# The second attention's filling matmuls in passes of 384 columns and two PSUM banks, with VectorE's order changed

## The chip, the cores and the metric
The kernel runs on one core of one Trainium2 chip. The metric is device time in microseconds (us). The engines are TensorE (PE), VectorE (DVE), ScalarE (ACT), GpSimd (POOL) and SyncE (SP); each runs its own instructions in order and waits for the others by semaphores. PSUM, where TensorE writes its products, has eight banks of 512 fp32 columns.

## The reference
Two layers of a diffusion backbone over 512 latent tokens and 256 context tokens, 1024 wide. Each layer runs three token mixers on one modulated input, merges them by sigmoid gates, projects, and then runs a SwiGLU. The part that matters is mixer B, a neighbourhood attention of eight heads of 64 with a learned bias, and context keys in the same softmax:

```
qa, ka, va, qb, kb, vb, uc, gz = jnp.split(h @ w_in, IN_SPLITS, axis=-1)
s_nb = jnp.einsum('bqhd,brqjhd->bhqrj', q_r, k_win).astype(jnp.float32) * scale
s_nb = s_nb + bias[None].astype(jnp.float32)
s_ctx = jnp.einsum('bqhd,bshd->bhqs', q_r, kc).astype(jnp.float32) * scale
s = jnp.concatenate([s_nb.reshape(B, H, GRID_W, kr * kcn), s_ctx], axis=-1)
p = jax.nn.softmax(s, axis=-1).astype(v.dtype)
y = ga * (oa @ w_branch[0]) + gb * (ob @ w_branch[1]) + gf * (oc @ w_branch[2])
```

The last layer has no output for the context, so there queries and gates are 512 tokens wide, and keys still 768.

## The kernel before
Products keep fp32's precision by parts: each operand is split into a high part (fp32r) and the rest, the low part, and three matmuls stand for one. A weight unit is 128 output columns; ScalarE makes its high part (line 587), GpSimd its low part (line 513).

The second attention (`attention` with `branch == 1`) is a loop of slots. A slot n is one head and one pair of query tiles: three slots a head in layer 0 (two with latent queries and one with context queries, `ORDER`), two in layer 1. "Odd" and "even" head mean its number. In a slot TensorE does, in this order:
- the scores of slot n + 1 into banks 0 to 3 (line 2005), for its first and its second query tile;
- the turn (transpose) of slot n's probabilities in up to three groups, into banks 4 and 3 in turn (line 2036). The first group waits for GpSimd's `p_ready`, the product of the exponentials with the inverse row sums (line 525);
- half of the slot's filling matmuls (`fill`, line 2091), a last small turned group, the output products (line 2055), the other half of the filling matmuls, and the output product of the last group.

The filling matmuls work off eight weight units beside the attention: six are queries and keys of the coming heads, alternately (0, 2, 4 queries, 1, 3, 5 keys), the last two are gates. A 768-wide unit takes 24 steps of two matmuls, 384 columns into bank 6 and 384 into bank 7; a 512-wide one takes 24 matmuls into bank 6. One unit is spread over three slots in layer 0 and two in layer 1. The first matmul of a unit waits until the one before is read out: ScalarE writes the high parts (`query_parts`, line 747, or `key_parts`, line 755) and VectorE the low parts (`query_rest`, line 1422, or `key_rest`, line 1431) from the same banks.

In a slot ScalarE also takes half of the output out of PSUM (`move_half`, line 893), the high parts of the turned groups (`turned_hi`, line 870), the exponentials of slot n + 1 (`probs`, line 862), and for odd heads the output's high part (`out_hi`, line 900), whose low part GpSimd makes between its two products (`o_rest`, line 533). At the end of a slot in which a unit ended it splits a weight unit, and after a key unit it copies the key rows to the other half of the partitions (`key_copies`, line 763). The scores of the first slot of each second head wait for these copies and for the low parts. Then it starts the bias transfer of the next head. VectorE does the fold of the output (`fold`, line 1518), the maxima of slot n + 1 (`maximum`, lines 1465 to 1479), the low parts of the turned groups (`turned_lo`, line 1493) and the inverses of the row sums (line 1486).

The order of each engine is written out by hand in the loop over n; no scheduler moves it.

## Time and profile before

| | us |
|---|---|
| median of 3 runs | 2493.85 |
| lowest, highest | 2493.56, 2496.89 |
| the profiled execution | 2498.33 |
| its span, first to last instruction | 2496.5 |
| TensorE busy in the span | 2315.2 (93%) |
| second attention, layer 0 | 548 to 722 of the span |
| second attention, layer 1 | 1845 to 1984 of the span |

The profile is one execution. A row of waits says who waited, for whom, and for how long. A row of the timeline says when an instruction (or a few alike) began, how long it took, and in brackets how long its engine had been idle and who ended that. Matmuls overlap, so the start of the next tells more than the length. PE's granted clock is given as a share of full speed.

### The profile page before, as it was taken

The numbers are of one execution on the slowest core, as the hardware profiler recorded it, in microseconds if no ns is written. First come the engines' busy times: TensorE is split into PE (matmuls) and PEld (weight loads), VectorE is DVE, ScalarE is ACT, GpSimd is POOL, SyncE is SP. The second block draws the span as 40 slices with busy tenths as digits, with TensorE's granted clock in tenths as the row PEclk, the third lists the DMA queues.
The fourth block names the chain that finished last, engine by engine and source line by source line (L and its number), as shares of the span: only waits on it lengthen the run. The fifth ranks groups of instructions, "written<-read, shape, count | busy, mean of one in ns | idle before, by whom it ended". The sixth has DMA issues, their size and how long they took to land. (4 is left out here: it accounts for less than half of the span.)

```text
span 2496.5 us, 34770 instructions
## 1 busy us (share of the span) xinstructions
PE 2315.2 (93%) x13090; PEld 2107.2 (84%) x13090; DVE 1222.7 (49%) x2548; ACT 949.3 (38%) x1852; POOL 1088.3 (44%) x844
## 2 busy tenths in 40 slices
PE   6989999998899989999999979899998898999997
PEld 2879888987789989999999868778877788988887
DVE  5786266565543474663831274546635526311124
ACT  3222366435541562111111244256535536422223
POOL 1333255434443544333532433446434456644545
PEclk9989999999999999999999989999999999999999
DMA  6541100132112535443522533121222245533335
GB/s 244 193 139 51 51 26 26 43 137 58 58 45 74 181 130 190 134 154 107 171 90 67 161 101 122 54 64 35 65 67 66 66 152 161 152 94 99 110 117 170
DMA packets 117935, 263.86 MB, mean 106 GB/s; under 512 B 13348, under 2 KB 13604, under 8 KB 116136
## 3 DMA queue, kind: packets, MB, share of 16 engines
q1 hardware_dynamic: 108000, 233.89, 29.6%
q10 hardware_dynamic: 9800, 28.19, 3.4%
q8 instruction: 82, 1.34, 0.2%
q14 instruction: 53, 0.43, 0.1%
HBM read 251.53 MB, written 10.49 MB: 105 GB/s over the span
## 5 line engine op out<-in xcount | busy, mean ns | idle before, releaser
L513 POOL TENSOR_TENSOR w_lo<-raw,w_hi 128x512 fp32r<-128x512 f32 x632 | 864.8, 1390 | 1031.2 <-ACT w_hi L587 1030.6
L587 ACT ACTIVATE w_hi<-raw 128x512 fp32r<-128x512 f32 x632 | 366.8, 626 | 682.8 <-PE ps L1747 251.1
L525 POOL TENSOR_TENSOR p_sb<-p_sb,row_inv 128x768 f32<-128x768 f32 (+2 forms) x160 | 185.3, 1168 | 300.7 <-DVE row_inv L1486 300.0
L1745 PE MATMUL ps<-h_hi,w_lo 128*128 128x384 f32 (+1 forms) x864 | 311.4, 360 | 1.2 <-DVE h_lo L1244 1.2
L1745 PE MATMUL ps<-h_lo,w_hi 128*128 128x384 f32 (+1 forms) x864 | 311.1, 360 | 0.0
L1745 PE MATMUL ps<-h_hi,w_hi 128*128 128x384 f32 (+1 forms) x864 | 311.1, 360 | 0.0
L1576 DVE TENSOR_TENSOR ps<-silu_g,ps 128x768 f32<-128x768 f32 (+3 forms) x52 | 37.8, 726 | 379.4 <-PE ps L1747 177.5
L1745 PEld LDWEIGHTS ps<-h_hi,w_lo 128*128 128x128 f32 x864 | 162.2, 188 | 17.3 <-DVE h_lo L1244 1.4
L1745 PEld LDWEIGHTS ps<-h_lo,w_hi 128*128 128x128 f32 x864 | 162.2, 188 | 16.0
L1745 PEld LDWEIGHTS ps<-h_hi,w_hi 128*128 128x128 f32 x864 | 162.2, 188 | 15.9
L2091 PE MATMUL ps<-h_hi,w_lo 128*128 128x384 f32 (+1 forms) x408 | 134.3, 364 | 27.1 <-DVE k_ll L1431 14.8
L1747 PE MATMUL ps<-h_hi,w_hi 128*128 128x384 f32 x456 | 152.3, 334 | 0.0
L1747 PE MATMUL ps<-h_lo,w_hi 128*128 128x384 f32 x456 | 152.3, 334 | 0.0
L1747 PE MATMUL ps<-h_hi,w_lo 128*128 128x384 f32 x456 | 152.3, 334 | 0.0
L870 ACT ACTIVATE pt_hi<-ps 128x512 fp32r<-128x512 f32 (+1 forms) x208 | 114.3, 550 | 97.7 <-PE ps L2036 96.3
L1104 DVE SCALAR_TENSOR_TENSOR ada_unused_gate_up<-ada_raw_gate_up,ada_cond_gate_up 128x1024 bf16<-128x1024 f32 x96 | 143.2, 1491 | 5.3 <-DMA ada_raw_gate_up<-in_w_ada 0.3
L1493 DVE TENSOR_TENSOR pt_lo<-ps,pt_hi 128x512 fp32r<-128x512 f32 (+1 forms) x208 | 129.5, 624 | 21.6 <-ACT pt_hi L870 20.3
L862 ACT ACTIVATE p_sb<-ps,neg_max 128x768 f32<-128x768 f32 (+2 forms) x160 | 120.4, 753 | 35.6 <-DVE neg_max L1479 19.1
L2091 PE MATMUL ps<-h_lo,w_hi 128*128 128x384 f32 (+1 forms) x408 | 132.0, 359 | 0.0
L2091 PE MATMUL ps<-h_hi,w_hi 128*128 128x384 f32 (+1 forms) x408 | 131.9, 358 | 0.0
L2036 PE MATMUL ps<-ident,p_sb 128*128 128x128 f32 x736 | 108.8, 280 | 20.2 <-DVE pt_lo L1493 16.7
L2036 PEld LDWEIGHTS ps<-ident,p_sb 128*128 128x128 f32 x736 | 84.8, 141 | 42.8 <-DVE pt_lo L1493 36.3
(219 smaller groups left out, 5474.4 us busy)
## 6 DMA issues: line engine op xcount, KB each, us to landing
raw<-in_stream SPq DMA_DIRECT2D x632, 256.0 KB, 2.8
ada_raw_gate_up<-in_w_ada SPq DMA_DIRECT2D x48, 512.0 KB, 3.6
ada_raw_fourier_in<-in_w_ada SPq DMA_DIRECT2D x24, 512.0 KB, 4.4
bias_sb<-in_bias ACTq DMA_DIRECT2D x32, 320.0 KB, 3.0
first_raw<-in_w_first SPq DMA_DIRECT2D x8, 1152.0 KB, 5.2
scratch<-xr ACTq DMA_DIRECT2D x16, 512.0 KB, 3.8
xr<-scratch SPq DMA_DIRECT2D x14, 512.0 KB, 4.9
ln_rows<-in_norm_rows SPq DMA_DIRECT2D x8, 512.0 KB, 5.2
```

The lines of the kernel that those rows point to most:

```text
L513: nc.gpsimd.tensor_tensor(w_lo[:, u % 2, cols], raw[:, u % 2, cols], w_hi[:, u % 2, cols].bitcast(F32), ALU.subtract).then_inc(S("lo_made" ...
L525: nc.gpsimd.tensor_tensor(p, p, row_inv[:, c:c + 1].broadcast_to([P, keys]), ALU.mult).then_inc(S("p_ready"), 1)
L587: nc.scalar.activation(w_hi[:, s, cols], raw[:, s, cols], ACT.Copy).then_inc(S("hi_made"), 1)
L862: nc.scalar.activation(p_sb[branch][n % 2][i][:, 0:keys], region(branch, i, 0, keys), ACT.Exp, bias=neg_max[:, i:i + 1], accum_out=row_sum ...
L870: nc.scalar.activation(pt_hi[branch][:, a:a + w], ps[:, TURN_BANK[branch] + order % 2, 0:w], ACT.Copy).then_inc(S("hi_out"), 1)
L1104: nc.vector.scalar_tensor_tensor(ada_unused[kind][:, :], ada_raw[kind][:, s, :], 1.0, ada_cond[kind][:, c, :], ALU.mult, ALU.mult, accum_o ...
L1493: nc.vector.tensor_tensor(pt_lo[branch][:, a:a + w], ps[:, TURN_BANK[branch] + order % 2, 0:w], pt_hi[branch][:, a:a + w].bitcast(F32), AL ...
L1576: nc.vector.tensor_tensor(up, shaped(silu_g[:, c, 0:w]), up, ALU.mult).then_inc(S("hidden"), 1)
L1745: last = nc.tensor.matmul(bank(0), tile, x[:, k, 0:split], start=start, stop=stop)
L1747: last = nc.tensor.matmul(bank(1), tile, x[:, k, HALF:TOK], start=start, stop=stop)
L2036: last = nc.tensor.transpose(ps[:, TURN_BANK[branch] + order % 2, col:col + P], p_sb[branch][n % 2][i][:, a:a + P], ident[:, :])
L2091: last = nc.tensor.matmul(ps[:, bank, 0:b - a], tile, x[:, k, a:b], start=r == 0, stop=r == FILL_STEPS - 1, skip_group_check=True)
```

## The change
- The unit's work is cut into passes (`fill_passes`): a 768-wide unit is two passes of 24 matmuls with 384 columns, a 512-wide one stays one pass. The number of matmuls stays as it was; a unit's weight tiles are now gone through once for each pass. Pass after pass the bank alternates between 6 and 7 (`pass_bank`), and the first matmul of a pass waits for the pass before the last.
- High and low parts are taken for each pass (64x384 instead of 64x768), the first pass's at a time of its own: `first_pass_ended` tells in which slot, "late" in layer 0 (behind everything else of the slot) and "early" in layer 1.
- VectorE's order in the second attention becomes: first maximum, low part of the first turned group, fold, low part of the second group, second maximum, first inverse, low parts of a pass, second inverse, last group, a late pass.
- ScalarE takes a pass's high parts ahead of `move_half`, and `out_hi` moves from before the second exponential to behind the last turned group.

The first attention (`branch == 0`) keeps its order and its passes.

```
+                    if branch == 1:
+                        if n + 1 < count:
+                            maximum(n + 1, 0)
+                        turned_lo(n, 0)
+                        if n:
+                            fold(n - 1)
+                        for g in groups[1:2]:
+                            turned_lo(n, g)
+                        if n + 1 < count:
+                            maximum(n + 1, 1)
+                            invert(n + 1, 0)
+                        if f is not None:
+                            fill_rest(f, len(fill_passes(ph, f)) - 1)
+                        if early is not None:
+                            fill_rest(early, 0)
+                        if n + 1 < count:
+                            invert(n + 1, 1)
+                        for g in groups[2:]:
+                            turned_lo(n, g)
+                        if late is not None:
+                            fill_rest(late, 0)
+                        continue
...
                     if f is not None:
-                        fill_out(f)
+                        fill_out(f, len(fill_passes(ph, f)) - 1)
+                    if early is not None:
+                        fill_out(early, 0)
+                    if branch == 1 and n:
+                        move_half(n - 1)
...
                     for g in groups[2:]:
                         turned_hi(n, g)
+                    if branch == 1 and n and (n - 1) // pairs % 2:
+                        out_hi(n - 1)
                     for name in slot_pieces(ph, n):
                         piece(*name)
+                    if late is not None:
+                        fill_out(late, 0)
...
                         if r == 0:
-                            if f or half:
-
-                                pe.wait_ge(S("fill_out"), at(ph, "fill_out") + fill_halves(ph) * f + half)
+                            held = 2 if branch == 1 else 1
+                            if m >= held:
+
+                                pe.wait_ge(S("fill_out"), at(ph, "fill_out") + m - held + 1)
                                 if branch == 1:
-                                    pe.wait_ge(S("fill_lo"), at(ph, "fill_lo") + min(f, 6))
+                                    pe.wait_ge(S("fill_lo"), at(ph, "fill_lo") + min(m - held + 1, passes_to(ph, 6)))
...
-                            runs = ((6, 0, HALF), (7, HALF, TOK)) if wide else ((6, 0, LAT),)
-                        for bank, a, b in runs:
-                            last = nc.tensor.matmul(ps[:, bank, 0:b - a], tile, x[:, k, a:b], start=r == 0, stop=r == FILL_STEPS - 1,
-                                                    skip_group_check=True)
+                        last = nc.tensor.matmul(ps[:, bank, 0:b - a], w[:, u % 2, k * P:(k + 1) * P], x[:, k, a:b], start=r == 0,
+                                                stop=r == FILL_STEPS - 1, skip_group_check=True)
...
+def fill_passes(ph, f):
+
+    if ph.tiles > LT or ph.part and f < 6 and f % 2:
+        return ((0, HALF), (HALF, TOK))
+    return ((0, LAT),)
+
+def passes_to(ph, f):
+
+    return sum(len(fill_passes(ph, n)) for n in range(f))
+
+def pass_bank(ph, f, i):
+
+    return FILL_BANK[ph.part] + (passes_to(ph, f) + i) % 2 if ph.part else FILL_BANK[0]
+
+def first_pass_ended(ph, n, late):
+
+    f, part = divmod(n + 2, ph.tiles // 2)
+    if part == 1 and f < FILLS and len(fill_passes(ph, f)) == 2 and late == (ph.tiles > LT):
+        return f
+    return 0 if n == 0 and not late and len(fill_passes(ph, 0)) == 2 else None
```

VectorE in layer 0, the slot in which a key unit has just ended, before. `k_ll_115` holds the keys' low parts, `o_sum_117` the folded output, `max_c` and `neg_max` the maxima:

```order
L1518 TENSOR_TENSOR o_sum_117<-ps,o_half_119 64x256 [waits moved]
L1431 TENSOR_TENSOR k_ll_115<-ps,k_hh_113 64x768 [waits fill_out]
L1431 TENSOR_TENSOR k_ll_115<-ps,k_hh_113 64x768
L1476 TENSOR_REDUCE max_c<-ps 128x1 [waits scored]
L1479 TENSOR_SCALAR neg_max<-max_c 128x1 [waits max_part]
L1476 TENSOR_REDUCE max_c<-ps 128x1 [waits scored]
L1479 TENSOR_SCALAR neg_max<-max_c 128x1 [waits max_part]
L1493 TENSOR_TENSOR pt_lo_131<-ps,pt_hi_129 128x512 [waits hi_out]
L1486 RECIPROCAL row_inv<-row_sum 128x1 [waits probs]
L1493 TENSOR_TENSOR pt_lo_131<-ps,pt_hi_129 128x512 [waits hi_out]
L1486 RECIPROCAL row_inv<-row_sum 128x1 [waits probs]
L1493 TENSOR_TENSOR pt_lo_131<-ps,pt_hi_129 128x128 [waits hi_out]
```

The same slot of the changed kernel, on the same engine:

```order
L1476 TENSOR_REDUCE max_c<-ps 128x1 [waits scored]
L1479 TENSOR_SCALAR neg_max<-max_c 128x1 [waits max_part]
L1493 TENSOR_TENSOR pt_lo_131<-ps,pt_hi_129 128x512 [waits hi_out]
L1518 TENSOR_TENSOR o_sum_117<-ps,o_half_119 64x256 [waits moved]
L1493 TENSOR_TENSOR pt_lo_131<-ps,pt_hi_129 128x512 [waits hi_out]
L1476 TENSOR_REDUCE max_c<-ps 128x1 [waits scored]
L1479 TENSOR_SCALAR neg_max<-max_c 128x1 [waits max_part]
L1486 RECIPROCAL row_inv<-row_sum 128x1 [waits probs]
L1431 TENSOR_TENSOR k_ll_115<-ps,k_hh_113 64x384 [waits fill_out]
L1431 TENSOR_TENSOR k_ll_115<-ps,k_hh_113 64x384
L1486 RECIPROCAL row_inv<-row_sum 128x1 [waits probs]
L1493 TENSOR_TENSOR pt_lo_131<-ps,pt_hi_129 128x128 [waits hi_out]
```

The keys' low parts moved from ahead of the maxima to between the inverses, and the second maximum from ahead of both low parts of the turned groups to behind them.

ScalarE in that slot, before (`k_hh_113` the keys' high parts, `p_sb` the probabilities, `pt_hi_129` the turned ones):

```order
L893 ACTIVATE o_half_119<-ps 64x256 [waits folded,attended]
L755 ACTIVATE k_hh_113<-ps 64x768 [waits unit_done]
L755 ACTIVATE k_hh_113<-ps 64x768
L870 ACTIVATE pt_hi_129<-ps 128x512 [waits turned_p]
L862 ACTIVATE p_sb_126,row_sum<-ps,neg_max 128x256 [waits turned_p,max_ready]
L870 ACTIVATE pt_hi_129<-ps 128x512 [waits turned_p]
L900 ACTIVATE o_sb<-o_sum_117 128x256 [waits folded]
L862 ACTIVATE p_sb_127,row_sum<-ps,neg_max 128x256 [waits turned_p,max_ready]
L870 ACTIVATE pt_hi_129<-ps 128x128 [waits turned_p]
L587 ACTIVATE w_hi<-raw 128x512 [waits raw_ready10,unit_done]
L587 ACTIVATE w_hi<-raw 128x512 [waits raw_ready11]
L763 ACTIVATE k_hh_113<-k_hh_113 64x768 [waits fill_out]
```

And of the changed kernel (its lines 754, 892, 869, 861, 899 and 762 are the old 755, 893, 870, 862, 900 and 763):

```order
L754 ACTIVATE k_hh_113<-ps 64x384 [waits unit_done]
L754 ACTIVATE k_hh_113<-ps 64x384
L892 ACTIVATE o_half_119<-ps 64x256 [waits folded,attended]
L869 ACTIVATE pt_hi_129<-ps 128x512 [waits turned_p]
L861 ACTIVATE p_sb_126,row_sum<-ps,neg_max 128x256 [waits turned_p,max_ready]
L869 ACTIVATE pt_hi_129<-ps 128x512 [waits turned_p]
L861 ACTIVATE p_sb_127,row_sum<-ps,neg_max 128x256 [waits turned_p,max_ready]
L869 ACTIVATE pt_hi_129<-ps 128x128 [waits turned_p]
L899 ACTIVATE o_sb<-o_sum_117 128x256 [waits folded]
L587 ACTIVATE w_hi<-raw 128x512 [waits raw_ready10,unit_done]
L587 ACTIVATE w_hi<-raw 128x512 [waits raw_ready11]
L762 ACTIVATE k_hh_113<-k_hh_113 64x768 [waits fill_out]
```

The output's high part moved behind the last turned group; the splitting of the weights and the key copies still stand behind all of it. GpSimd's order is unchanged.

## Rows read from the trace of the kernel before

**Rows 1.** Line 2091, the filling matmuls: what ended their idle time (us, times).
```profile
  DVE k_ll L1431: 14.8, 6
  DVE q_st L1422: 11.6, 6
```
**Rows 2.** Timeline of PE, layer 0: turns of seven slots (start, length, us).
```profile
608.85 1.04 PE L2036 MATMUL ps<-ident,p_sb 128*128 128x128 f32 x8
618.27 0.60 PE L2036 MATMUL ps<-ident,p_sb 128*128 128x128 f32 x4
624.20 1.03 PE L2036 MATMUL ps<-ident,p_sb 128*128 128x128 f32 x8
630.11 1.04 PE L2036 MATMUL ps<-ident,p_sb 128*128 128x128 f32 x8
640.84 0.60 PE L2036 MATMUL ps<-ident,p_sb 128*128 128x128 f32 x4
646.99 1.09 PE L2036 MATMUL ps<-ident,p_sb 128*128 128x128 f32 x8
653.03 1.04 PE L2036 MATMUL ps<-ident,p_sb 128*128 128x128 f32 x8
```
**Rows 3.** Timeline of PE, layer 1: turns of five slots, and of the last two.
```profile
1869.23 1.03 PE L2036 MATMUL ps<-ident,p_sb 128*128 128x128 f32 x8
1880.08 1.04 PE L2036 MATMUL ps<-ident,p_sb 128*128 128x128 f32 x8
1886.75 1.03 PE L2036 MATMUL ps<-ident,p_sb 128*128 128x128 f32 x8
1896.60 1.04 PE L2036 MATMUL ps<-ident,p_sb 128*128 128x128 f32 x8
1904.36 1.04 PE L2036 MATMUL ps<-ident,p_sb 128*128 128x128 f32 x8
...
1972.54 1.03 PE L2036 MATMUL ps<-ident,p_sb 128*128 128x128 f32 x8
1977.74 1.97 PE L2036 MATMUL ps<-ident,p_sb 128*128 128x128 f32 x8 [0.83 <-POOL p_sb L525]
```
**Rows 4.** Timeline of all engines, layer 0, one slot of an odd head.
```profile
602.80 1.09 PE L2036 MATMUL ps<-ident,p_sb 128*128 128x128 f32 x8
603.50 0.60 ACT L870 ACTIVATE pt_hi<-ps 128x512 fp32r<-128x512 f32 x1 [2.58 <-PE ps L2036]
603.60 0.41 DVE L1465 TENSOR_REDUCE max_c<-ps 128x1 f32<-128x256 f32 x1
...
604.65 0.60 ACT L870 ACTIVATE pt_hi<-ps 128x512 fp32r<-128x512 f32 x1
604.65 0.21 DVE L1473 TENSOR_SCALAR neg_max<-max_a,max_c 128x1 f32<-128x1 f32 x1
...
605.43 0.81 ACT L862 ACTIVATE p_sb<-ps,neg_max 128x640 f32<-128x640 f32 x1
605.45 0.67 DVE L1493 TENSOR_TENSOR pt_lo<-ps,pt_hi 128x512 fp32r<-128x512 f32 x1
...
606.36 0.17 DVE L1486 RECIPROCAL row_inv<-row_sum 128x1 f32<-128x1 f32 x1 [0.24 <-ACT p_sb L862]
606.61 0.73 POOL L533 TENSOR_TENSOR o_sb<-o_sum,o_sb 128x256 fp32r<-128x256 f32 x1
...
607.31 1.25 POOL L525 TENSOR_TENSOR p_sb<-p_sb,row_inv 128x640 f32<-128x640 f32 x1
```
**Rows 5.** Tile k_ll: low parts of the first attention (ns: least, median, most).
```profile
L1508 DVE TENSOR_TENSOR k_ll<-ps,k_hh x16: 417/556/695, 297.4 to 1687.1; 64x512 fp32r<-64x512 f32 x8, 64x256 fp32r<-64x256 f32 x8
```
**Rows 6.** Timeline of ACT and PE, layer 0, a key unit's copies and the scores.
```profile
681.66 1.70 ACT L763 ACTIVATE k_hh<-k_hh 64x768 fp32r<-64x768 f32 x2
683.46 0.48 PE L2005 MATMUL ps<-k_hh,q_st 128*128 128x256 f32 x2 [0.71 <-issue]
```
**Rows 7.** A stretch behind a fill wait: PE, PEld, DVE, ACT, POOL busy, clock.
```profile
590.80:594.60 3.80, 3.80 (x18) 3.57 (x17) 1.84 (x6) 3.76 (x11) 2.96 (x4) 0.55 0.30 84
```

More of the change, by code:

```diff
@@ L942, in attention @@
                     f = fill_ended(ph, n - 1)
-                    if n:
+                    early, late = (first_pass_ended(ph, n, late) if branch == 1 else None for late in (False, True))
+                    if branch == 0 and n:
                         move_half(n - 1)
                     if f is not None:
-                        fill_out(f)
+                        fill_out(f, len(fill_passes(ph, f)) - 1)
[3 more added lines that the diff above has]
+                        move_half(n - 1)
                     turned_hi(n, 0)
@@ L951, in attention @@
                         turned_hi(n, g)
-                    if fill_halves(ph) == 2 and (n + 1) % pairs == 0 and n + 1 < count:
-                        gate_half((n + 1) // pairs, 0)
-                    if n and (n - 1) // pairs % 2:
+                    if branch == 0 and ph.tiles > LT and (n + 1) % pairs == 0 and n + 1 < count:
+                        fill_out((n + 1) // pairs, 0)
+                    if branch == 0 and n and (n - 1) // pairs % 2:
                         out_hi(n - 1)
@@ L1430, in key_rest @@
                     rows, n = slice(HD * x, HD * x + HD), 2 * (c % 2) + x
-                    last = nc.vector.tensor_tensor(halves(k_ll[1][rows, n, :], TOK), product(qk_bank(c, 1), TOK, rows),
-                                                   halves(k_hh[1][rows, n, :].bitcast(F32), TOK), ALU.subtract)
+                    last = nc.vector.tensor_tensor(halves(k_ll[1][rows, n, a:b], w), product(bank, w, rows),
+                                                   halves(k_hh[1][rows, n, a:b].bitcast(F32), w), ALU.subtract)
                 last.then_inc(S("fill_lo"), 1)
@@ L1540, in attention @@
                     f = fill_ended(ph, n - 1)
+                    early, late = (first_pass_ended(ph, n, late) if branch == 1 else None for late in (False, True))
+                    if branch == 1:
[20 more added lines that the diff above has]
+                        continue
                     if n:
                         fold(n - 1)
[L1543 to L1548 removed]
                     if n + 1 < count:
```

111 lines of the change are left out of this document (48 added, 63 removed).

## The prediction
> **What bounds the kernel now.** I read the shares of busy time first, then who waits for whom in the second attention alone, then its instructions in order of time, since only those tell which wait ends last. Over the whole program TensorE is busy 93%, so most stages have nothing to give. In the second attention it is not: there the filling matmuls are released late by VectorE's low parts, six times 14.8 us in all for keys and six times 11.6 us for queries [rows 1]. These 26.4 us are what the change can take away at its source, and no more than that can come from this edit.
>
> The stage runs in slots, one per head and pair of query tiles: scores of the next slot, turns of this slot's probabilities, half of the filling matmuls, output products, the other half. I measure a slot from one turn's start to the next. In layer 0 a head has three slots: 9.42, 5.93 and 5.91 us for a head with an even number and 10.73, 6.15 and 6.04 for an odd one [rows 2]. In layer 1 four slots make a period: 10.85, 6.67, 9.85 and 7.76 us [rows 3]. The long ones are those in which a new unit starts.
>
> **The fill wait (gone).** With two banks in turn, a pass needs the pass before the last to be read out, and that happened most of a slot ago. ScalarE's and VectorE's reading of the last pass lies beside this slot's matmuls. So TensorE's idle time at the fill goes in all 12 places. I take it whole; the question is what is late next.
>
> **The new order's chain.** Before, VectorE did both maxima first and the low parts after. Now the second maximum stands behind both low parts, and the second half of the probabilities behind it on ScalarE. From one slot [rows 4], laid in the new order from the turn's start: 0.70 to the first high part, 1.15 to the second's start, 0.60 for it, 0.67 for its low part, 1.26 for the second maximum (603.60 to 604.86), 0.93 from the second exponential's start to the inverse, 0.15 and 0.08 to GpSimd, 1.25 for its product, 0.06 to the next turn. That is 6.85, about 6.8 us, since an instruction begins a little before the one ahead ends. Where the high part of the output is due, it now stands behind the last turned group: 0.4 on ScalarE and 0.7 on GpSimd, queued ahead of the second product there (the order of GpSimd's queue has not moved), so 7.8 us. Before, such a slot took 5.9 to 6.1 us, because nothing of the second maximum hung on the turn. This is a loss of 0.9 to 1.8 us in each slot that had no fill wait to lose.
>
> **The low parts of a pass.** 64x512 takes 695 ns and 64x256 417 [rows 5], so 64x384 should take 556 and a pass of two 1.1 us. It stands between the two inverses. In slots with context keys it is covered. In the last slot of an even head in layer 0 VectorE still has 0.4 us of the late pass's low parts to do when the slot begins, so the first maximum moves and the slot takes 7.3 instead of 6.8.
>
> **The key copies.** ScalarE doubles a unit's key rows at the end of the slot, behind the splitting of a weight unit. The scores of the next head pair wait for it. In the trace this already ends last: the copies end at 683.36 and the scores start at 683.46, with 0.71 us idle before [rows 6]. The change moves them little: second exponential at about 4.4 us (3.7 in layer 0, whose next scores are the short context ones), 0.9 to the end of the last high part, 1.2 of splitting, 1.7 of copies, so they end at 8.2 (7.5). Then 0.1 and the scores' 1.1 (four pairs like the row at 683.46): the slot takes 9.4 in layer 1 and 8.75 in layer 0. That is the wait that takes the place of the fill's in each key unit.
>
> **The sum, layer 0.** Even head: first slot 6.5 (TensorE's own work: the third slot's 5.91, and 0.6 since the next scores are the long ones; so the fill wait was 2.9), second 5.95 (GpSimd's product just in time), third 7.3; 19.75 against 21.26, so -1.5, three times -4.5. Odd head: 8.75, 6.75 (5.95 and the output's high part), 7.75; 23.25 against 22.92, so +0.3, three times +1.0. The very first slot and the last two heads have no fill wait to lose, yet pay the chain: I take +4.2, of which the last short slots are the larger part, as in layer 1 below. Sum +0.7 us.
>
> **The sum, layer 1.** 10.85 becomes 9.4, 6.67 becomes 7.8, 9.85 becomes 7.9 (chain with output) and 7.76 becomes 7.7 (TensorE's work, the last low part just late): 32.8 against 35.13, -2.3, three times -7.0. The end has slots without filling work: 5.20 us between the last turns [rows 3] becomes 7.0, and two before it lose 0.3 each: +2.4. Sum -4.6 us.
>
> Together -3.9 us. The profiled execution took 2498.33 us (span 2496.5), 4.5 above the median of the runs, 2493.85; its own sum gives 2494.4, which is 2490 beside the median. Of the 26.4 us taken away some 22 come back, 6 at the key copies and the rest along the chain of the second maximum. A measurement of this kernel can tell about 0.2% (5 us) from no change, so this is "the same", 2488.9 to 2498.8.
>
> **The clock.** Just behind the fill wait of an odd head TensorE's granted clock fell to 0.55 for 3.8 us [rows 7], that is mostly the lower of its two levels. An odd head's first slot took 10.73 instead of 9.42 [rows 2], so such a stretch costs 1.3 us. I count three of them in the two stages. My sum lets these stretches vanish with the waits. The longest idle time that I leave is some 2.1 us, ahead of the scores behind the key copies.
> The Trainium skill (TensorE: Matmul & The Clock Gate, section "A second HAM failure mode: psum-queue depth-cycling") tells of a kernel that cycles through PSUM banks, in which many short idle times between groups of matmuls made the clock fall and rise over and over. By that rule this change, which trades few long waits for many short ones, is the wrong way round, and its case is the third rival. That short waits do it no row here shows: in the rows the fall follows a long one.
>
> **Rivals.**
> First, the late chain is hidden and only the key copies stay: slots then run at TensorE's work. For it speaks that my chain adds handoffs one by one, each read from a slot in which something else may have been waited for. Against it: GpSimd's product is needed whole before the turn and already ends 0.06 us ahead of it in odd heads. It gives 2493.85 - 26.4 + 9 (six key copies at 1.5) = 2476.
> Second, on the other side, the second maximum costs more than I read. It is ahead of both the exponential and the product in about 34 of 40 slots. Each 0.25 us that the low parts, the fold between them or the start of the maximum add per slot is 8.5 us: 2490 + 8.5 = 2498.5, and at 0.4 us it is 2504. It decides from 0.26 us a slot on. For it: the first low part cannot begin before the first maximum has ended, and where the maximum waits for a bias transfer the whole chain moves. Against it: all its pieces are read with their handoffs, from a slot in which only GpSimd's product ended late.
> Third, the clock falls in each of the 12 units, where before three stretches were slow in these stages: and my sum let those vanish. Twelve at 1.3 us are 15.6: 2490 + 16 = 2506.
> Fourth, the change does not do what it says, since the pass before the last is not yet read out when a new one starts. Then the fill waits stay and the chain is paid in full: 2493.85 + 22 = 2516. Against it: the first pass of a unit ends a whole slot before the next unit begins.
>
> **How the numbers follow.** The forecast has 0.45, and alone it reaches from 2482 to 2498 (0.2 us a slot either way on 40 slots): 0.17 of its chance lies below 2488.9, 0.24 within, 0.04 above. The first rival has 0.23, all faster. The second has 0.18, of which 0.04 is within. The third has 0.11 and the fourth 0.03, both slower. That is 0.40 faster, 0.28 the same and 0.32 slower. The time is the forecast's, 2490. The range holds the forecast, most of the first rival and the second, and the near part of the third: 2473 to 2507.
>
> **What would show it.** Right: in the waits of the second attention no filling matmul waits for q_st or k_ll; turns wait for GpSimd's p_sb in most slots, and scores for the copies of k_hh (about 2 us, six times); an odd head's slots in layer 0 add up to some 23 us, an even one's to 20, a period in layer 1 to 33. Wrong: turns seldom wait for p_sb and the periods shrink to TensorE's work (first rival); slots of 7.3 or more everywhere (second); a granted clock under 0.95 in both stages (third); fill waits still there (fourth). All other stages must keep their times within 1 us.

## The result and the profile after

| | us |
|---|---|
| before, median of 7 runs | 2494.06 (2492.42 to 2500.57) |
| changed, median of 7 runs | 2504.86 (2501.92 to 2507.62) |
| ratio, 95% interval | 1.0037 [1.0026, 1.0049] |
| forecast | 2490.0 (2473 to 2507) |
| changed, the profiled execution, its span | 2501.92, 2500.1 |
| TensorE busy in the span | 2330.5 (93%) |

The changed kernel is slower by 10.8 us, where the forecast was 4 us faster. The profiled executions are only 3.6 us apart in span, since that of before lies 4.3 us above its median and that of the changed kernel 2.9 below its own. So stages are compared below, not spans.

**The wait is gone.** These are rows from the page's list of costliest groups. The filling matmuls (now line 2109) have 0.7 us of idle time ahead of them in the whole program, and none of it for k_ll or q_st [rows 1]. The line of the exponential (861, before 862) has become the one that waits. Changed kernel:

```profile
L2109 PE MATMUL ps<-h_hi,w_lo 128*128 128x384 f32 (+1 forms) x408 | 149.3, 366 | 0.7 <-ACT gates_a L911 0.7
L861 ACT ACTIVATE p_sb<-ps,neg_max 128x768 f32<-128x768 f32 (+2 forms) x160 | 120.3, 752 | 76.6 <-DVE neg_max L1473 58.2
```
The same line of ScalarE in the kernel before:
```profile
L862 ACT ACTIVATE p_sb<-ps,neg_max 128x768 f32<-128x768 f32 (+2 forms) x160 | 120.4, 753 | 35.6 <-DVE neg_max L1479 19.1
```
The exponentials' idle time went from 35.6 to 76.6 us. That is the late second maximum, read in one row; m2 below, which moves it alone, has 7.6.

**The slots, layer 0.** Turns of the changed kernel on TensorE, to be laid beside [rows 2]; the start of one less that of the one ahead is a slot:

```profile
601.09 1.10 PE L2060 MATMUL ps<-ident,p_sb 128*128 128x128 f32 x8 [1.36 <-POOL p_sb L525]
609.01 1.09 PE L2060 MATMUL ps<-ident,p_sb 128*128 128x128 f32 x8 [1.04 <-POOL p_sb L525]
615.68 0.60 PE L2060 MATMUL ps<-ident,p_sb 128*128 128x128 f32 x4
621.65 1.09 PE L2060 MATMUL ps<-ident,p_sb 128*128 128x128 f32 x8 [0.43 <-POOL p_sb L525]
629.11 1.09 PE L2060 MATMUL ps<-ident,p_sb 128*128 128x128 f32 x8
638.43 1.05 PE L2060 MATMUL ps<-ident,p_sb 128*128 128x128 f32 x4
646.03 1.09 PE L2060 MATMUL ps<-ident,p_sb 128*128 128x128 f32 x8 [1.47 <-POOL p_sb L525]
```
An even head is 6.67, 5.97 and 7.46 us (20.1; before 21.26), an odd one 9.32, 7.60 and 7.92 (24.8; before 22.92); the 7.92 ends with the turn at 653.95, shown further down. Turns now wait for GpSimd's product, as the bracket says.

**The slots, layer 1**, beside [rows 3]:

```profile
1868.69 1.04 PE L2060 MATMUL ps<-ident,p_sb 128*128 128x128 f32 x8
1876.09 1.04 PE L2060 MATMUL ps<-ident,p_sb 128*128 128x128 f32 x8
1885.47 1.04 PE L2060 MATMUL ps<-ident,p_sb 128*128 128x128 f32 x8
1893.38 1.09 PE L2060 MATMUL ps<-ident,p_sb 128*128 128x128 f32 x8 [0.46 <-POOL p_sb L525]
1901.22 1.10 PE L2060 MATMUL ps<-ident,p_sb 128*128 128x128 f32 x8
...
1975.78 1.03 PE L2060 MATMUL ps<-ident,p_sb 128*128 128x128 f32 x8
1982.58 1.97 PE L2060 MATMUL ps<-ident,p_sb 128*128 128x128 f32 x8 [0.60 <-POOL p_sb L525]
```
A period is 7.40, 9.38, 7.91 and 7.84: 32.5 us, before 35.1.

**One slot in order of time**, from 601.09 to 609.01, beside [rows 4]; start and length in us:

```profile
602.42 0.69 DVE L1493 TENSOR_TENSOR pt_lo<-ps,pt_hi 128x512 fp32r<-128x512 f32 x1
603.14 0.43 DVE L1518 TENSOR_TENSOR o_sum<-ps,o_half 64x256 f32<-64x256 f32 x1
603.68 0.69 DVE L1493 TENSOR_TENSOR pt_lo<-ps,pt_hi 128x512 fp32r<-128x512 f32 x1
604.29 0.41 DVE L1465 TENSOR_REDUCE max_c<-ps 128x1 f32<-128x256 f32 x1
...
605.59 0.80 ACT L861 ACTIVATE p_sb<-ps,neg_max 128x640 f32<-128x640 f32 x1 [1.94 <-DVE neg_max L1473]
...
606.50 0.17 DVE L1486 RECIPROCAL row_inv<-row_sum 128x1 f32<-128x1 f32 x1 [0.88 <-ACT p_sb L861]
606.53 0.41 ACT L899 ACTIVATE o_sb<-o_sum 128x256 fp32r<-128x256 f32 x1
...
607.02 0.73 POOL L533 TENSOR_TENSOR o_sb<-o_sum,o_sb 128x256 fp32r<-128x256 f32 x1 [0.28 <-ACT o_sb L899]
...
607.71 1.25 POOL L525 TENSOR_TENSOR p_sb<-p_sb,row_inv 128x640 f32<-128x640 f32 x1
```
The second exponential begins 4.50 us behind the turn (the chain said 4.4), and GpSimd's second product, ready to go at 606.7, starts at 607.71 behind the output's sum. The slot is 7.92; the chain said 7.8.

**The waits in layer 1** (1868 to 1984 us), in all, times, longest:

```profile
ACT p_sb L861 <- DVE neg_max L1473: 27.3, 14, 2.0
DVE max_c L1465 <- DMA bias_sb<-in_bias: 10.2, 7, 1.7
PE ps L2029 <- issue: 5.5, 3, 1.8
```
Layer 0 has the first and the last of these alike (27.0 and 5.5 us), and no wait for the bias transfer. The last is the scores behind the key copies. In time, beside [rows 6]:

```profile
1882.54 1.70 ACT L762 ACTIVATE k_hh<-k_hh 64x768 fp32r<-64x768 f32 x2
1884.33 0.47 PE L2029 MATMUL ps<-k_hh,q_st 128*128 128x256 f32 x2 [1.84 <-issue]
```

**The clock.** The windows run from a layer's first turn to 12 us behind its last; the pairs are busy time of PE, PEld, DVE, ACT and POOL, and the last three numbers are granted clock, DMA share and GB/s. Before, then changed:

```profile
558.90:731.07 172.17, 143.55 (x919) 133.41 (x918) 99.96 (x295) 96.72 (x225) 71.73 (x75) 0.98 0.18 52
1852.30:1989.74 137.44, 114.71 (x686) 101.47 (x685) 78.63 (x232) 78.25 (x172) 59.42 (x55) 0.95 0.22 65
```
```profile
557.24:736.12 178.88, 152.02 (x899) 135.17 (x898) 101.46 (x304) 97.70 (x235) 72.38 (x74) 0.94 0.17 50
1860.94:1994.58 133.64, 117.14 (x685) 101.93 (x684) 80.83 (x237) 77.89 (x178) 59.80 (x54) 0.95 0.23 67
```
Length times the missing share of the clock is 3.4 + 6.9 = 10 us before and 10.7 + 6.7 = 17 after (each clock is rounded to 0.01, so each product is good to 1 us). Five of the seven us more are lost behind layer 0's last turn (12 us at 0.57). The same 12 us before and in the changed kernel:

```profile
722.00:734.00 12.00, 12.00 (x71) 12.00 (x70) 7.87 (x9) 4.78 (x7) 3.44 (x4) 1.00 0.16 48
```
```profile
722.00:734.00 12.00, 8.70 (x32) 8.11 (x33) 2.00 (x5) 6.76 (x14) 5.57 (x7) 0.57 0.14 45
```
From the last turn to the next stage's first gate product, before and changed, is 7.1 us (719.07 to 726.14) and 10.5 (724.12 to 734.64):

```profile
726.14 0.96 DVE L1405 TENSOR_TENSOR ps<-gate_b,ps 128x768 f32<-128x768 f32 x1 [3.33 <-PE ps L1747]
```
```profile
734.64 0.96 DVE L1404 TENSOR_TENSOR ps<-gate_b,ps 128x768 f32<-128x768 f32 x1 [5.44 <-PE ps L1771]
```

### The profile page after: what moved, and what is told of

Same layout as the page of the kernel before. It is cut to its first block and busy times, and to the rows that moved or that the text cites. A ratio compares the mean times of both kernels' runs of the same rounds, so it can differ in the third digit from the quotient of the medians.

```text
span 2500.1 us, 34819 instructions
## 1 busy us (share of the span) xinstructions
PE 2330.5 (93%) x13090; PEld 2113.3 (85%) x13090; DVE 1230.2 (49%) x2566; ACT 952.0 (38%) x1872; POOL 1086.3 (43%) x844
## 5 line engine op out<-in xcount | busy, mean ns | idle before, releaser
L1769 PE MATMUL ps<-h_hi,w_lo 128*128 128x384 f32 (+1 forms) x864 | 311.4, 360 | 1.2 <-DVE h_lo L1243 1.2
L1769 PE MATMUL ps<-h_lo,w_hi 128*128 128x384 f32 (+1 forms) x864 | 311.1, 360 | 0.0
L1769 PE MATMUL ps<-h_hi,w_hi 128*128 128x384 f32 (+1 forms) x864 | 311.1, 360 | 0.0
L2109 PE MATMUL ps<-h_hi,w_lo 128*128 128x384 f32 (+1 forms) x408 | 149.3, 366 | 0.7 <-ACT gates_a L911 0.7
L861 ACT ACTIVATE p_sb<-ps,neg_max 128x768 f32<-128x768 f32 (+2 forms) x160 | 120.3, 752 | 76.6 <-DVE neg_max L1473 58.2
L2109 PE MATMUL ps<-h_lo,w_hi 128*128 128x384 f32 (+1 forms) x408 | 146.2, 358 | 0.0
L2109 PE MATMUL ps<-h_hi,w_hi 128*128 128x384 f32 (+1 forms) x408 | 146.1, 358 | 0.0
```

Source lines behind the costliest of these rows:

```text
L861: nc.scalar.activation(p_sb[branch][n % 2][i][:, 0:keys], region(branch, i, 0, keys), ACT.Exp, bias=neg_max[:, i:i + 1], accum_out=row_sum ...
L1769: last = nc.tensor.matmul(bank(0), tile, x[:, k, 0:split], start=start, stop=stop)
L2109: last = nc.tensor.matmul(ps[:, bank, 0:b - a], w[:, u % 2, k * P:(k + 1) * P], x[:, k, a:b], start=r == 0, stop=r == FILL_STEPS - 1, skip ...
```

## The experiments

Sixteen kernels (one of them the changed kernel again) in four groups of four, each group beside runs of the kernel before (medians 2494.64, 2495.66, 2496.25 and 2495.18). The table has the median, the ratio to before, the sum of the slots of both layers (first to last turn) and the clock lost, worked out as above.

| kernel | us | ratio, interval | slots | clock lost |
|---|---|---|---|---|
| before (first profile) | 2494.06 | | 285.6 | 10 |
| changed | 2504.86 | 1.0037 [1.0026, 1.0049] | 288.5 | 17 |
| a1 changed again | 2502.82 | 1.0028 [1.0018, 1.0037] | 289.3 | 19 |
| p1 passes only | 2491.37 | 0.9985 [0.9977, 0.9994] | 279.3 | 12 |
| m2 maxima first | 2468.02 | 0.9886 [0.9871, 0.9900] | 255.0 | 7 |
| k1 copies first | 2492.75 | 0.9989 [0.9981, 0.9998] | 279.1 | 10 |
| m1 late maximum | 2519.96 | 1.0101 [1.0086, 1.0115] | 307.6 | 21 |
| r1 old vector order | 2503.65 | 1.0034 [1.0021, 1.0047] | 291.6 | 15 |
| d1 bias early | 2501.12 | 1.0021 [1.0011, 1.0032] | 288.3 | 17 |
| b2 all three | 2464.38 | 0.9873 [0.9859, 0.9887] | 251.0 | 3 |
| f1 fold first | 2472.39 | 0.9913 [0.9899, 0.9927] | 261.4 | 5 |
| p2 old scalar order | 2473.33 | 0.9911 [0.9897, 0.9924] | 258.3 | 5 |
| e1 one low ahead | 2494.67 | 0.9999 [0.9988, 1.0009] | 281.3 | 9 |
| o1 output early | 2496.14 | 1.0003 [0.9992, 1.0013] | 281.6 | 13 |
| t1 end as before | 2500.23 | 1.0021 [1.0011, 1.0030] | 283.7 | 17 |
| h1 rests behind inverses | 2508.32 | 1.0056 [1.0043, 1.0070] | 294.3 | 14 |
| c3 only maximum late | 2485.20 | 0.9973 [0.9959, 0.9987] | 272.6 | 7 |
| b3 all four | 2466.51 | 0.9884 [0.9869, 0.9899] | 252.4 | 6 |

**p1.** The changed kernel, with VectorE's and ScalarE's old orders in the second attention:

```diff
-  maximum(n+1, 0); turned_lo(n, 0); fold(n-1); turned_lo(n, 1)
-  maximum(n+1, 1); invert(n+1, 0); fill_rest(...); invert(n+1, 1)
+  fold(n-1); fill_rest(...); maximum(n+1, 0); maximum(n+1, 1)
+  turned_lo(n, 0); invert(n+1, 0); turned_lo(n, 1); invert(n+1, 1)
```
ScalarE's old order is the one written out under p2.

> The changed kernel's passes and banks, with VectorE's and ScalarE's old order in the second attention (fold, a pass's low parts, both maxima, then the turned groups; output's high part before the second exponential). Theory A, the loss is the second maximum behind the low parts: the fill waits stay away and no chain comes in their place, so slots without a unit's start stay at 5.9 to 6.2 us, an even head in layer 0 takes 18.5 to 19, a period of four slots in layer 1 about 31, and the time is 2470 to 2480, 14 to 24 under the kernel before. Theory B, the passes themselves cost (twice the instructions for the parts, the changed order of the weight tiles): no faster than 2492. Theory C, TensorE's clock: fewer waits, so it must have less time at the lower level than the changed kernel.

It gained 3 us, far less than the 14 to 24 of theory A; theory B's bound was 2492. TensorE lost 12 us of clock and not 17, as theory C wanted. The fill wait is gone, but with two passes a unit's low parts come twice, and in the old order they stand ahead of the maxima. VectorE in layer 1, one slot:

```profile
1879.84 0.43 DVE L1514 TENSOR_TENSOR o_sum<-ps,o_half 64x256 f32<-64x256 f32 x1 [2.07 <-ACT o_half L892]
1881.06 1.39 DVE L1417 SCALAR_TENSOR_TENSOR q_st<-ps,q_st 64x512 fp32r<-64x512 f32 x2 [0.79 <-ACT q_st L746]
...
1884.86 0.68 DVE L1489 TENSOR_TENSOR pt_lo<-ps,pt_hi 128x512 fp32r<-128x512 f32 x1
```
The turn began at 1880.34, and its first low part only 4.5 us later; TensorE's second group waits 2.12 us for that. One slot of each period of four in layer 1 (7.43, 7.76 and 7.41 us before) takes 9.38 here.

**m2.** The changed kernel with one edit:

```diff
   maximum(n+1, 0)
+  maximum(n+1, 1)
   turned_lo(n, 0); fold(n-1); turned_lo(n, 1)
-  maximum(n+1, 1)
```


> The changed kernel with the second maximum put directly behind the first on VectorE, nothing else moved. Theory A: the second exponential and GpSimd's product come early again, turns no longer wait for p_sb, the first low part starts some 0.6 us later. 2478 to 2488. Theory B: at most 3 us under the changed kernel, 2501 to 2506.

35 to 37 us faster than the changed kernel (its two medians) and 1.1% faster than before: 10 us below the range of theory A. The exponentials' idle time fell from 76.6 to 7.6:

```profile
L861 ACT ACTIVATE p_sb<-ps,neg_max 128x768 f32<-128x768 f32 (+2 forms) x160 | 120.5, 753 | 7.6 <-DVE neg_max L1479 7.1
```
The same slot as above, in m2: the turn at 600.26, the second exponential 2.33 us behind it, the second product at +5.49 instead of +6.62:
```profile
600.26 1.09 PE L2060 MATMUL ps<-ident,p_sb 128*128 128x128 f32 x8
...
602.59 0.80 ACT L861 ACTIVATE p_sb<-ps,neg_max 128x640 f32<-128x640 f32 x1
...
605.75 1.25 POOL L525 TENSOR_TENSOR p_sb<-p_sb,row_inv 128x640 f32<-128x640 f32 x1
```

**k1.** The changed kernel with the copies ahead of the split:

```diff
+  key_copies(f // 2 + 1, ...)
   act.wait_ge(S("unit_done"), ph.unit + f + 1)
   split(ph.unit + f + 2, f % 2)
-  key_copies(f // 2 + 1, ...)
```

> The changed kernel with the key copies ahead of the splitting of the weight unit on ScalarE. If the scores' wait for the copies is what ends last in the six key slots, each gets 1.1 us shorter (odd heads of layer 0 from 24.8 to 23.7 us, periods in layer 1 from 32.6 to 31.5): 2497 to 2500. If the late chain behind it takes the place of the wait, no gain: 2503 to 2506.

A gain of 10 to 12 us against the changed kernel, about twice what was expected. The six waits are not gone but down from 1.8 us to 0.8:

```profile
1875.82 0.47 PE L2029 MATMUL ps<-k_hh,q_st 128*128 128x256 f32 x2 [0.80 <-issue]
```
Slots without slow clock give back the same 1.04 us (9.38 to 8.34 in layer 1, 8.79 to 7.75 in layer 0), as was expected: 6.2 in six. The slots give back 9.4 to 10.2 in all. The other 3 to 4 are stretches of lower clock: the changed kernel has five among its slots, k1 two. The copies were a bound, as the prediction said, and the clock came back on top.

**a1.** The changed kernel, unchanged, among the others.

> The changed kernel once more, for a second profile beside the others: 2503 to 2507. If the 4 us that the two profiles leave unexplained are the clock elsewhere, the stage in layer 0 again costs about 10 us more than before and that in layer 1 about 3.5 less, while the time at the lower clock in other stages differs.

2502.8, at the fast end of what was expected. Layer 0's stage, first turn to gate product, again costs 10.2 us more than before. Layer 1's costs 1.6 less and not 3.5, as the clock is low for 10.5 us behind its last turn, where the first profile has 7. The stretches of lower clock among the slots are again five, one of them at another place (609 us, where the first profile has 637).

**m1.** The kernel before, with the second maximum late on VectorE in the second attention. The first inverse moves with it, to where the changed kernel has it:

```diff
   maximum(n+1, 0)
-  maximum(n+1, 1)
   turned_lo(n, 0)
-  invert(n+1, 0)
   turned_lo(n, 1)
+  maximum(n+1, 1); invert(n+1, 0)
   invert(n+1, 1)
```

> The kernel before with one edit: in the second attention VectorE takes the second maximum of the next pair behind both low parts of the turned probabilities instead of directly behind the first maximum. Units stay one reading of 768 columns, nothing else moves. Theory A (the late second maximum is what makes the changed kernel slower, and does so by itself): the 25 or so slots without a wait for a unit's reading go from 5.9 to 6.8 us or more, the slots with such a wait absorb part of it: 2508 to 2520 us. Theory B (it costs only together with the passes' own work on VectorE): within 4 us of before, 2491 to 2498.

24 us slower than before, at the top of theory A's range: the late maximum costs without the passes too. The slots grew by 22 and the clock lost doubled from 10 to 21, so part of the 24 is slow clock. The first inverse's share was not run by itself. In the changed kernel it stays late in m2, which gains 35 us all the same.

**r1, f1.** Two VectorE orders between the changed kernel's with maxima first (m2) and p1's, with ScalarE's new order.

```diff
+  fold(n-1)                        # r1 and f1
+  fill_rest(...)                   # r1 alone
   maximum(n+1, 0); maximum(n+1, 1); turned_lo(n, 0)
+  invert(n+1, 0)                   # r1 alone
-  fold(n-1)                        # r1 and f1
   turned_lo(n, 1)
-  invert(n+1, 0)                   # r1 alone
-  fill_rest(...)                   # r1 alone
   invert(n+1, 1)
```

> The changed kernel with VectorE's old order (fold, rests of the pass, both maxima, then low parts) but ScalarE's new order. The kernel with the passes and both old orders took 2491.4 us, the changed one with both maxima first 2468.0. Theory A (VectorE's work ahead of the maxima, the fold and above all the rests of 1.1 to 1.4 us, took the 23 us between these two): 2487 to 2493. Theory B (ScalarE's order took them: output halves moved ahead of the first high part and the output's high part ahead of the second exponential): 2466 to 2473.

> The kernel with the passes and both maxima first (2468.0 us) with one edit on VectorE: the fold of the last output stands ahead of the maxima again, as in the kernel before; the passes' low parts stay between the two inverses. With the whole of VectorE's old order (fold and low parts of the pass ahead of the maxima) it took 2503.7, and there the fold waits 15 times, 55.9 us in all in layer 1, for ScalarE's first half of the output. Theory A (this wait, at the head of VectorE's queue, makes most of the 36 us between the two): 2485 to 2500. Theory B (the low parts of a pass, 1.1 to 1.4 us ahead of the maxima, make it): 2469 to 2476.

f1 is 4 us from m2, r1 36. So the fold at the head of the queue costs 4 us, though in r1's layer 1 it waits 55.9 us in all, and the low parts of a pass ahead of the maxima (with the first inverse early again) cost 31. The 4 us are near what the medians can tell (the intervals of f1 and m2 just meet), but the slots grow too, from 255.0 to 261.4. f1 is theory B; theory A had taken the largest wait in the list for the cause, and it was a place where VectorE waited anyway. r1 missed both its ranges, being 12 us above p1: ScalarE's new order is bad together with VectorE's old one.

**p2.** m2 with ScalarE's old order:

```diff
+  move_half(n-1)
   fill_out(...)
-  move_half(n-1)
   turned_hi(n, 0); probs(n+1, 0); turned_hi(n, 1)
+  out_hi(n-1)
   probs(n+1, 1); turned_hi(n, 2)
-  out_hi(n-1)
```

> The kernel with the passes and both maxima first (2468.0 us) with ScalarE's old order: first half of the output ahead of the pass's high parts, the output's high part ahead of the second exponential. Behind VectorE's old order this was worth -12 us (2491.4 against 2503.7), as the fold was then waited for. Theory A (only the fold at the head of VectorE's queue made ScalarE's order matter, and the fold is now behind the first low part): 2465 to 2471. Theory B (ScalarE's new order costs by itself): 2455 to 2461.

2473.3, in neither range: with the maxima first, ScalarE's new order is worth 5 us (first and third slot of an odd head in layer 0: 7.94 and 7.40 us, in m2 7.38 and 6.80).

**d1.** The changed kernel with the bias transfer earlier on ScalarE:

```diff
+  load_bias(ph, h + 1, j)
   fill_out(...); ...; split(...); key_copies(...)
-  load_bias(ph, h + 1, j)
```

> The changed kernel with one edit: ScalarE issues the transfer of the next head's bias at the start of the slot instead of at its end, behind split and key copies. In the trace of the changed kernel the maxima wait 7 times for this transfer in the layer with it, 10.2 us in all, and it takes 2.8 us to land. Theory A (those waits lie on the chain from maximum to turn): 2493 to 2498, against 2504 of the changed kernel. Theory B (the scores' second half or the low parts are ready no earlier than the bias, so the waits are hidden or change their name): 2501 to 2505.

2501.1, theory B: 2 to 4 us, at the edge of what can be told. The seven waits of 10.2 us are gone from the trace, but they had mostly covered others; layer 1's slots went from 121.6 to 121.3.

**b2.** The edits of m2, k1 and d1 together.

> The changed kernel with three edits together: both maxima ahead of the low parts, key copies ahead of the split of the weights, bias transfer issued at the slot's start. With the maxima alone it took 2468.0. Theory A (with the maxima early, the slots are bound by TensorE, and the scores wait only 2.6 us in all for key copies, the maxima once for a bias, 2.8 us): 2463 to 2467. Theory B (the edits add up as the copies did on the changed kernel, 10 to 12 us): 2452 to 2458.

2464.4, theory A, and the fastest of all, 1.3% under before. TensorE's clock does not fall at all in layer 1:

```profile
1838.56:1957.05 118.49, 112.00 (x691) 98.92 (x690) 78.52 (x239) 78.28 (x178) 60.81 (x55) 1.00 0.25 72
```

**e1.** The changed kernel with one low part less ahead of the second maximum:

```diff
   maximum(n+1, 0); turned_lo(n, 0); fold(n-1)
+  maximum(n+1, 1)
   turned_lo(n, 1)
-  maximum(n+1, 1)
```

> The changed kernel with the second maximum of VectorE behind the first low part and the fold, ahead of the second low part: half of the delay of the changed kernel, which took 2504, against 2468 with both maxima first. Theory A (each part of the chain counts as long as it is: the low part of 0.67 us ahead of the maximum is about half of what stands there): 2482 to 2490. Theory B (a threshold: up to some delay GpSimd's product is in time behind TensorE's work, so the first half costs little): 2468 to 2476.

2494.7, neither. Taking one low part away gives back 8 to 10 of 36 us; a low part and the fold still ahead of the maximum cost 27, three quarters of the whole. The expectation called this half of the delay, and it is more. In the slot shown for the changed kernel and m2 the second exponential starts 3.94 us behind the turn (598.46), where those have 4.50 and 2.33:

```profile
602.40 0.80 ACT L861 ACTIVATE p_sb<-ps,neg_max 128x640 f32<-128x640 f32 x1 [1.38 <-DVE neg_max L1473]
```
That is 74% of the way from m2 to the changed kernel, and 68% over all slots of both layers. The price goes roughly with the delay, once the delay is read where the exponential starts.

**o1.** The changed kernel with the output's high part where it was before:

```diff
+  out_hi(n-1)
   probs(n+1, 1); turned_hi(n, 2)
-  out_hi(n-1)
```

> The changed kernel with the output's high part on ScalarE ahead of the second exponential again. The prediction charged its new place, behind the last high part, with up to 1 us in the slots where it is due (GpSimd's sum of it stands ahead of the second product in its queue). Theory A (this charge is right, 12 to 16 such slots, some of them bound by other things): 2493 to 2499. Theory B (ahead of the exponential it costs ScalarE's chain its 0.4 us, and GpSimd's product is not late by the other way): 2501 to 2506.

7 to 9 us, theory A: the charge for its place was right.

**t1.** The changed kernel, maxima together in the last slots of each layer alone:

```diff
   maximum(n+1, 0)
+  if count - pairs - 2 <= n < count - 1: maximum(n+1, 1)
   turned_lo(n, 0); fold(n-1); turned_lo(n, 1)
-  maximum(n+1, 1)
+  if n < count - pairs - 2: maximum(n+1, 1)
```

> The changed kernel with the second maximum directly behind the first in the last four or five slots of each layer alone (the last of them have no filling work). In the changed kernel the last slots of layer 0 take 6.27, 5.96, 6.86 and 6.22 us against 6.35, 5.93, 5.91 and 4.36 before, and behind them TensorE's granted clock is at its lower level for 10.5 us, where before it did not fall. Theory A (the fall follows from the longer idle time ahead of the last turns): the slots give back 2.8 us in layer 0 and 2 in layer 1, the clock 3.4 more: 2494 to 2498. Theory B (the fall at the end of the stage comes anyway): 2499 to 2501, and the lower clock is seen at the end of layer 0 again.

2500.2, theory B. The last four slots of layer 0 give back 1.7 us (6.26, 5.95, 6.20 and 5.21 against 25.31 in all) and the last three of layer 1 2.0, but the clock falls behind layer 0 all the same:

```profile
722.00:729.50 7.50, 6.07 (x21) 6.07 (x22) 1.55 (x3) 4.26 (x7) 2.76 (x4) 0.54 0.25 72
```

**h1.** The changed kernel with a pass's low parts behind both inverses:

```diff
   invert(n+1, 0)
+  invert(n+1, 1)
   fill_rest(...)
-  invert(n+1, 1)
   turned_lo(n, 2)
```

> The changed kernel with the low parts of a pass (1.1 us on VectorE) behind the second inverse instead of between the two. Theory A (as the prediction said, in slots with context keys they are covered by the second exponential): 2501 to 2506. Theory B (they end behind the exponential, and the inverse and GpSimd's product wait for them in some dozen slots): 2492 to 2498.

2508.3, slower than both ranges. Layer 1's slots grew by 5 us (126.6 against 121.6). There the pass's low parts now run behind the inverse, so the turned low part of the slot's last group is late, and TensorE with it:

```profile
1881.84 1.10 DVE L1431 TENSOR_TENSOR k_ll<-ps,k_hh 64x384 fp32r<-64x384 f32 x2
...
1882.98 0.29 DVE L1493 TENSOR_TENSOR pt_lo<-ps,pt_hi 128x128 fp32r<-128x128 f32 x1
...
1883.32 0.33 PE L2079 MATMUL ps<-pt_lo,v_b 128*128 128x128 f32 x1 [1.53 <-DVE pt_lo L1493]
```
Between the inverses they were covered by the exponential all but 0.2 us, as the prediction had it: with them out of the way GpSimd's second product starts 5.49 us behind the turn at 1868 and not 5.66, and no turn had waited for it there.

**c3, b3.** c3 is the changed kernel with the edits of k1, d1 and o1; b3 is c3 with m2's edit too.

> The changed kernel with all that proved better but the second maximum: key copies ahead of the split, bias transfer at the slot's start, the output's high part ahead of the second exponential. Alone these gave 12, 3 and 8 us against the changed kernel's 2504. Theory A (they lie in different slots and add up): 2479 to 2484. Theory B (part of each was the same lower clock, that comes back only once): 2486 to 2491.

> The same with the second maximum directly behind the first too. With all of it but the output's high part it took 2464.4. Theory A (the output's sum on GpSimd ahead of the second product was late there as well): 2459 to 2462. Theory B (with the maxima early ScalarE is the one that is late, and the high part ahead of the second exponential costs its 0.4 us): 2465 to 2470. Against the kernel above, the late second maximum alone then costs 20 to 25 us by either.

b3 less c3 is 18.7 us: the late second maximum alone, with the other causes gone, where 20 to 25 was expected. Against the changed kernel c3 gives 20 where the three edits alone gave 12, 4 and 9, between the two theories. b3 is 2 us above b2, its theory B. The medians alone could not tell that, but the third slot of an odd head in layer 0 takes 7.40 and not 6.80 us: with the maxima first, the output's high part is better late.

## Why the prediction was wrong

**The fill wait goes** was right in all 12 places.

**The new order's chain** was right in its links: 4.50 us to the second exponential where 4.4 was said, slots of 7.92 where 7.8 was said, 5.97 where 5.95. By m1 it costs 24 us on the kernel before, where the prediction's fourth rival had 22; that they are so near is partly luck, since the 22 hold 6 of key copies and the 24 hold slow clock. That a pass's low parts are covered between the inverses (h1, all but 0.2 us) and the charge for the output's high part (o1) held too.

**The key copies** were right: 9.38 in layer 1 where 9.4 was said, 8.79 in layer 0 where 8.75 was.

**The sum, layer 1** was near: the slots took 3.8 us less than before, where -4.6 was said.

**The sum, layer 0** failed. It said +0.7 us. Measured from first turn to the next stage's gate product it is 177.4 us (557.24 to 734.64) against 167.2 (558.90 to 726.14): +10.2. Of the 9.5 us missed, 3.4 lie on the way from the last turn to the gate product, which my sum did not have at all. The three odd heads have 3.5 (24.59, 24.84 and 23.78 against 23.25), the three even ones 2.0 (20.08, 20.10 and 21.08 against 19.75). And 0.8 is mine: I took the odd heads of before at 22.92 each, and the two not in my rows were 22.77 and 22.23. The start and the last two heads were +3.9 (+4.2 said).

**The step that failed is the clock:** "My sum lets these stretches vanish with the waits." They did not: there are seven from the layers' first turns on, where before had four (the prediction counted three), and the clock lost went from 10 to 17 us. Four of the seven begin right at the scores behind the key copies, the very wait that the sum had kept as its longest. One of them, in the changed kernel:

```profile
636.75 0.47 PE L2029 MATMUL ps<-k_hh,q_st 128*128 128x256 f32 x2 [1.83 <-issue]
```
```profile
637.00:641.00 4.00, 4.00 (x19) 3.92 (x19) 1.86 (x6) 1.43 (x4) 0.74 (x1) 0.57 0.45 131
```
The clock over whole executions says the same as the two traces: its mean is 0.979 in 81 executions of the kernel before and 0.976 to 0.977 in 17 of the changed one, which is 6 to 7.5 us of 2500.

What a stretch costs is read between like slots of the changed kernel. The first two slots of an odd head are 9.07 and 7.60 or 9.32 and 7.60 with a stretch and 8.79 and 7.15 without, the first of an even head 7.67 with and 6.67 without. That is 0.7, 1.0 and 1.0 us, 2.7 in layer 0, and 3.4 more at its end: 6.1 of the 9.5 us are TensorE at the lower of its two levels. It is the third rival's mechanism at a part of its size. The 1.3 us of that rival was read between an odd and an even head. The kernel before has a third odd head without a stretch, 10.30 and 5.88 us in its first two slots, against 10.56 and 6.16 or 10.73 and 6.15 with one: 0.5 to 0.7. The chain itself is left with 0.5 us in an odd head (23.78 against 23.25) and 0.3 in an even one, 2.6 in six: too little to turn the sign by itself. Most of the odd head's is its second slot, 7.15 where 6.75 was said.

The 3.4 us at the end go with the clock in all eighteen profiles. The way from layer 0's last turn to the gate product takes 7.1 us in the two where the clock does not fall there (before and r1), 8.4 to 8.8 where it is low for 3.5 to 4 us (f1, p2, b3), 9.4 to 10.1 where it is low for 7 to 7.5 (ten kernels, p1, m1, m2 and b2 among them), and 10.4 to 10.5 where for 10 to 10.5 (changed, a1, d1). In b2, the fastest:

```profile
703.00:710.00 7.00, 5.11 (x18) 4.71 (x19) 1.55 (x3) 3.27 (x6) 3.87 (x4) 0.51 0.23 75
```
So this fall does not come from the late second maximum. Only about 1 us of the 3.4 sets the changed kernel apart from m2 and b2 (9.4 and 9.7).

The prediction said that no row shows short waits bringing the clock down. The changed kernel has such a row: at 654 the clock fell, and the waits of TensorE in the slot ahead are 1.47, 0.42 and 1.04 us, none as long as the 2.76 us ahead of the fall in [rows 7].

```profile
646.03 1.09 PE L2060 MATMUL ps<-ident,p_sb 128*128 128x128 f32 x8 [1.47 <-POOL p_sb L525]
651.95 0.33 PE L2079 MATMUL ps<-pt_lo,v_b 128*128 128x128 f32 x1 [0.42 <-DVE pt_lo L1493]
653.95 1.28 PE L2060 MATMUL ps<-ident,p_sb 128*128 128x128 f32 x6 [1.04 <-POOL p_sb L525]
```
```profile
654.00:658.00 4.00, 4.00 (x18) 3.97 (x19) 2.46 (x7) 1.88 (x5) 0.23 (x1) 0.57 0.02 4
```
The third odd head of the same execution has nearly the same three waits (1.45, 0.43 and 1.04) and no fall, and so has h1 at this place (1.47, 0.45 and 1.04), so they don't decide it alone. The Trainium skill (TensorE: Matmul & The Clock Gate, section "A second HAM failure mode: psum-queue depth-cycling") says that frequent short idle times between groups of matmuls are enough to make the clock swing. This trace agrees as far as the row at 654 goes, and the table by and large: b2 with the shortest slots lost 3 us, the changed kernel 17, m1 with the longest 21.

**What the prediction did not see** is the other half. "No more than that can come from this edit" held for the wait, not for the kernel: the 26.4 us were a bound on one wait. With the maxima first the rest of the change is worth 26 us (m2) and with the copies and the bias early 31 (b2), since the twelve slots with a fill wait held more of the old VectorE order's delays than the wait. In m2 these twelve are 36.9 us shorter than before, and the other 26 slots 6.3 longer; in the changed kernel the twelve are 21.9 shorter and the 26 are 24.8 longer. And the passes alone with the old orders are worth 3 (p1).

**What stays open.** In the profiled executions the two stages account for +6.7 us (10.2 in layer 0, -3.5 in layer 1 by the same marks), the medians differ by 10.8 (8 for a1). In a1's profile they account for +8.6, which is all of its 8. The remaining 2 to 4 us have no place in the first two traces, whose own scatter is as large. Why the clock falls behind layer 0's last turn in sixteen of the eighteen profiles, but not before and not in r1, was not settled; there is one profile of each, so the kernel before may have the fall in other executions. The clock cannot be held fixed here, so its share of the 18.7 us between c3 and b3 (lost clock 7 and 6) is small only by this measure. That slow clock is what the changed kernel's slots lost is read from like slots, not from a kernel in which nothing but the clock differs.

## What to carry to other kernels

When a wait is removed by reordering, look first at what the engine behind the reordered work waits for next: here the second maximum put behind two low parts of 0.7 us and the fold cost 19 to 37 us, and the change without that was worth 26. A wait in the list is not a price: 10.2 us of waiting for a transfer gave back 2 to 4, 55.9 us of waiting for the output's half gave 4, and 11 us behind the key copies, cut to 5, gave 10 to 12, of which 6 were the waits and most of the rest the clock. Don't count slow clock as something that goes with a wait while the sum keeps other waits: at 1.8 us they had a stretch behind them in four of six places, at 0.8 (k1) in one.

## What the runs showed of the hardware

TensorE's granted clock fell to its lower level behind waits no longer than 1.5 us (the rows at 646 to 658) and, in four of six places, right behind a wait of 1.8 us. It stayed low for 3.5 to 4 us inside the slots and mostly for 7 to 10.5 us at the end of a layer. Such a stretch among the slots cost 0.7 to 1.0 us in the changed kernel and 0.5 to 0.7 in the kernel before, not the 1.3 read before. At the end of layer 0, 7 us of it cost 2.3 to 3.0 us and 10.5 us cost 3.3 to 3.4, against the 7.1 us of the profiles without it. Equal waits do not always bring it: two places of one execution (the second and the third odd head of layer 0), and the same place in two executions (the changed kernel and h1 at 654), differ in whether it fell.
